# Projection banks asked for one at a time, a weight piece and zero products moved to the front, and a second early buffer for expert 2

## The reference

```python
def first_block(x, ...):
    hn = rms_norm(x, norm1_g)
    proj = hn @ w_in                       # 1024 -> 2304, the "projection" of this document
    # q and k are normed per head, some rotated; two attentions; w_out; conv FFN
    ...
def second_block(x, c, ctx, ...):
    # modulation by c, a scan and a windowed attention, then the experts:
    moe_x = hier_moe(h2, ...)              # 32 experts, 2 per token
    return rms_norm_2(x + g2 * moe_x, norm_final)

def expert_block(args):                    # for every expert e
    xb, e = args
    return (jax.nn.silu(xb @ w_gate[e]) * (xb @ w_up[e])) @ w_down[e]
```

## Time and profile before

| | us |
|---|---|
| median of 3 runs | 1606.25 (1605.87 to 1609.35) |
| the profiled execution | 1606.26 |
| its span on the chip | 1604.4 |
| PE busy | 1499.6 (93%) |

### The profile page before, as it was taken

One profiled execution on the slowest core, in us unless ns is written; L12 is line 12 of the kernel. 1 busy time (PEld: TensorE's weight loads), 2 busy tenths in 40 slices (PEclk: granted clock), 3 DMA queues, 4 the chain that ended last, 5 costly groups with the idle time before them and its releaser, 6 DMA issues.

```text
span 1604.4 us, 21206 instructions
## 1 busy us (share of the span) xinstructions
PE 1499.6 (93%) x8171; PEld 1041.4 (65%) x8171; DVE 913.7 (57%) x1697; ACT 518.9 (32%) x938; POOL 99.3 (6%) x132
## 2 busy tenths in 40 slices
PE   7999998999999999999999897988999999999896
PEld 6776667888888878878887686873444444344343
DVE  4745774467787567753764677472444454344435
ACT  5445665333343332243426534221101101010112
POOL 0000000000000000000004132001101101000100
PEclk9999998999999999999999999999999999999998
DMA  8212011255544357613020000565999999999993
GB/s 254 78 54 73 2 50 50 70 173 140 155 130 120 110 171 271 212 39 119 27 69 11 1 1 3 208 262 206 414 399 405 410 401 411 399 405 402 410 411 160
DMA packets 112365, 308.39 MB, mean 192 GB/s; under 512 B 13983, under 2 KB 65535, under 8 KB 90763
## 3 DMA queue, kind: packets, MB, share of 16 engines
q1 hardware_dynamic: 108755, 299.08, 50.4%
q0 software_dynamic: 3200, 7.87, 1.6%
q10 hardware_dynamic: 312, 0.10, 0.0%
HBM read 306.99 MB, written 4.22 MB: 194 GB/s over the span
## 4 chain that ended last, share of the span: by engine, by line
PE 73%; DMA 9%; DVE 8%; ACT 4%; issue 3%; SPq 2%; POOL 0%; DVEq 0%; ACTq 0%; POOLq 0%
PE bank L1309 68%; DMA arena<-in_w_up 8%; PE bank L1312 5%; SPq L826 1%; DVE arena L2192 1%; DVE ring L2134 0%; DVE hTc L2316 0%; ACT weights_high L971 0%; SPq L766 0%; DMA ring<-in_w_in 0%; DVE x_res L2205 0%; DVE ring L2136 0%; DVE xn L2204 0%; DVE arena L2386 0%; ACT hT_high L1031 0%
## 5 line engine op out<-in xcount | busy, mean ns | idle before, releaser
L1309 PE MATMUL bank<-weights_high,hT_high 128*128 128x512 f32 (+2 forms) x736 | 255.1, 385 | 12.6 <-ACT arena L1058 5.3
L1807 DVE TENSOR_TENSOR weights_low<-ring,weights_high 128x2048 fp32r<-128x2048 f32 (+2 forms) x61 | 135.6, 2224 | 139.8 <-ACT weights_high L971 138.9
L1309 PE MATMUL bank<-weights_low,hT_high 128*128 128x512 f32 (+2 forms) x560 | 212.6, 380 | 0.0
L971 ACT ACTIVATE weights_high<-ring 128x2048 fp32r<-128x2048 f32 (+2 forms) x61 | 113.4, 1859 | 190.7 <-PE bank L1309 158.0
L1309 PEld LDWEIGHTS bank<-weights_high,hT_high 128*128 128x128 f32 x736 | 139.0, 189 | 40.3 <-issue 8.4
L1309 PE MATMUL bank<-hT_high,weights_high 128*128 128x512 f32 x416 | 163.8, 394 | 0.8 <-DVE hT_low L1845 0.8
L1309 PE MATMUL bank<-hT_high,weights_low 128*128 128x512 f32 x416 | 161.9, 389 | 0.0
L1309 PE MATMUL bank<-hT_low,weights_high 128*128 128x512 f32 x416 | 161.9, 389 | 0.0
L2316 DVE TENSOR_TENSOR hTc<-bank,mod_gain 128x512 f32<-128x512 f32 x32 | 22.1, 691 | 193.9 <-PE bank L1312 193.9
L1309 PE MATMUL bank<-arena,hTc 128*64 128x512 f32 x496 | 115.6, 601 | 7.3 <-DMA arena<-in_w_up 5.7
L1309 PE MATMUL bank<-ring,hTc 128*64 128x512 f32 (+1 forms) x544 | 121.4, 583 | 0.6 <-DMA ring<-in_w_up 0.6
(11 more groups left out here) (329 smaller groups left out, 2483.7 us busy)
## 6 DMA issues: line engine op xcount, KB each, us to landing
arena<-in_w_up SPq DMA_DIRECT2D x32, 1024.0 KB, 20.0
arena<-in_w_down SPq DMA_DIRECT2D x16, 2048.0 KB, 22.3
ring<-in_w_gate SPq DMA_DIRECT2D x32, 1024.0 KB, 17.6
ring<-in_w_up SPq DMA_DIRECT2D x32, 1024.0 KB, 19.6
ring<-in_w_down SPq DMA_DIRECT2D x16, 2048.0 KB, 21.9
arena<-in_w_gate SPq DMA_DIRECT2D x30, 1024.0 KB, 18.6
xn<-in_w_ada SPq DMA_DIRECT2D x48, 512.0 KB, 4.7
ring<-in_w_up SPq DMA_DIRECT2D x44, 512.0 KB, 5.2
```

Of the source, the lines that this page charges most:

```text
L971: high_ready.tick(s.activation(part_view(w_high, key), raw_view(key), ACT.Copy), k)
L1309: return nc.tensor.matmul(o, lhsT, rhs, start=start, stop=stop)
L1807: low_ready.tick(v.tensor_tensor(part_view(w_low, key), raw_view(key), part_view(w_high, key), ALU.subtract), k)
```

## The change

Six edits. (1) The plan lists the projection's banks in the order in which they are first written, and PE opens each at its first matmul, not four together. (2) The nine products at n = 0 are gone. (3) POOL clears a 128x128 piece of `pj` at once, and PE multiplies it 15 times by itself before it waits for anything else. (4) SP issues the third weight piece after 10 of the small tables, ahead of the other 21. (5) Expert 2's up weights get a buffer of their own too (`early_up`, 16 KB per partition), loaded right after expert 1's weights and ahead of the store of the normed tokens; so expert 4's gate and up weights are loaded where expert 2's up weights were. (6) To make room, `ssd_small` lies in `early_up`, `convw` stands elsewhere, and the area for GpSimd's DMA descriptors is set to 4096 bytes.

```diff
+        early_up = sb("early_up", [P, UNIT])
...
+        sm = carve(0, 10, 96, of=early_up)
...
         for c in range(5):
             for n in range(4 * c, 4 * c + 4):
                 banks.plan(("proj", n), (pj_ready, n) if n < 16 else (v_tail, n - 16))
-
-            for n in range(4 * c - 2, 4 * c + 2):
-                if 0 <= n < 16:
+                if n % 2 and n >= 4:
+                    banks.plan(("qkT", 4 * c - 2 + n % 4 // 2), (qk_drained, 4 * c - 2 + n % 4 // 2))
+            if c < 4:
+                for n in range(4 * c, 4 * c + 2):
                     banks.plan(("qkT", n), (qk_drained, n))
...
                 if key == ("w_in", 1):
-                    for dst, src in small_loads[FIRST_LOADS:]:
+                    for dst, src in small_loads[FIRST_LOADS:FIRST_LOADS + 10]:
+                        sp.dma_start(dst, src).then_inc(more_in, 16)
+                if key == ("w_in", 2):
+                    for dst, src in small_loads[FIRST_LOADS + 10:]:
                         sp.dma_start(dst, src).then_inc(more_in, 16)
...
             load_expert(sp, 1, 1, None)
+            for half, landed in enumerate((first_in, second_in)):
+                sp.wait_ge(landed[1], 16)
+                load_rows(sp, 2, 0, 1, half, early_up[:, :])
             normed.wait(sp, ("norm2_2", TT - 1, 0))
             sp.dma_start(h_d.rearrange("(t p) n -> p t n", p=P), xn[:, 0:TT, :]).then_inc(h_stored, 16)
...
-            load_expert(sp, 2, 0, 1, True)
+            for landed in first_in[0:2] + second_in[0:2]:
+                sp.wait_ge(landed, 32)
+            load_gate_and_up(sp, 4, 0, 1)
+            load_down(sp, 2, 0, 1)
             load_expert(sp, 3, 1, 2)
             sp.wait_ge(gu_filled, 3)
             sp.dma_start(final_gain, inp["norm_final_2"].partition_broadcast(P)).then_inc(final_in, 16)
-            with sp.Fori(2, E // 2) as it:
+            load_down(sp, 4, 0, 3)
+            load_expert(sp, 5, 1, 4)
+            with sp.Fori(3, E // 2) as it:
...
+            g.memset(pj[:, 0, 0:P], 0.0).then_inc(zeros_ready, 1)
             banks.filled(pool, ("proj", len(PROJ) - 1))
...
+            opened = [banks.open(pe, ("hT",) + k) for k in halves("norm1")]
+            pe.wait_ge(zeros_ready, 1)
+            for _ in range(15):
+                mm(opened[0][:, 0:P], pj[:, 0, 0:P], pj[:, 0, 0:P], True, True)
             pe.wait_ge(const_in, CONST_ALL)
-            opened = [banks.open(pe, ("hT",) + k) for k in halves("norm1")]
...
                     bank = banks.open(pe, ("qkT", n))
-                    if n == 0:
-                        unread(bank, 9)
                     qk_ready.wait(pe, n)
...
-                opened = [banks.open(pe, ("proj", 4 * c + t)) for t in range(TT)] if c else []
+                opened = []
...
-                        if c == half == 0:
+                        if half == 0:
                             opened.append(banks.open(pe, ("proj", 4 * c + t)))
```

More of the change, by code:

```diff
@@ L195, in two_blocks @@
         gains = sb("gains", [P, 6, KT])
-        convw = sb("convw", [P, 224])
         ada_bias = sb("ada_bias", [P, 6, KT])
@@ L202, in two_blocks @@
         gates = sb("gates", [P, 2, D])
+        convw = sb("convw", [P, 224])
         dt_bias, a_log = sb("dt_bias", [P, 16]), sb("a_log", [P, 16])
@@ L294, in two_blocks @@
         skip_x = carve(2048 + 2 * (T + CTX), 512, of=slot)
-        sm = sb("ssd_small", [P, 10, 96])
         cat = xn
@@ L692, in two_blocks @@
         final_y = steps("final_y", range(TT))
+        zeros_ready = sem("zeros_ready")
         def pieces_of_turn(n):
@@ L766, in load_rows, with load_down, load_gate_and_up @@
             sp.dma_start(into[:, at], rows[:, at]).then_inc((first_in, second_in)[half][2 * par + i], 16)
-        def load_expert(sp, e, par, reuse, early=False):
+        def load_down(sp, e, par, reuse):
+            if reuse is not None:
+                sp.wait_ge(y_filled, reuse)
+            sp.dma_start(EXPERT_SLOTS[3 * par + 2], inp["w_down_2"].rearrange("a e (p f) d -> (a e) p (f d)", f=4)[e]).then_inc(
+                down_in[par], 16)
+        def load_gate_and_up(sp, e, par, reuse):
             if reuse is not None:
@@ L773, in load_expert @@
                 for i in range(2):
[L774 to L779, removed]
+                    load_rows(sp, e, par, i, half)
+        def load_expert(sp, e, par, reuse):
+            load_gate_and_up(sp, e, par, reuse)
+            load_down(sp, e, par, reuse)
         def modulation(sp, parts):
@@ L1709, in tokens_in_place, with gate_and_up @@
                 last.then_inc(xt_filled, 1)
-            def gate_and_up(n, par, kpar, gate=None):
-                gate_w, up_w = EXPERT_SLOTS[3 * par] if gate is None else gate, EXPERT_SLOTS[3 * par + 1]
+            def gate_and_up(n, par, kpar, early=None):
+                gate_w, up_w = EXPERT_SLOTS[3 * par:3 * par + 2] if early is None else early
                 pe.wait_ge(xt_ready, n + 1)
@@ L1774, in _ @@
                         pair_piece(pair, t)
-                gate_and_up(n, n % 2, n // 2, early_gate if n == 2 else None)
+                gate_and_up(n, n % 2, n // 2, (early_gate, early_up[:, :]) if n == 2 else None)
                 if n + 1 < E:
@@ L2399 @@
     from concourse.bass_utils import run_bass_kernel_spmd
-    nc = bacc.Bacc("TRN2", target_bir_lowering=False, num_devices=1)
+    nc = bacc.Bacc("TRN2", target_bir_lowering=False, num_devices=1, dynamic_dma_scratch_size=4096)
     arrays, aps = {}, {}
```

## The result

| | before | after |
|---|---|---|
| median of the runs | 1606.25 (5 runs, 1605.03 to 1609.35) | 1598.16 (5 runs, 1595.48 to 1598.88) |
| the profiled execution | 1606.26 | 1598.16 |
| its span | 1604.4 | 1596.2 |

The medians are 8.1 us apart, where 10.2 were forecast. The ratio of the runs is 0.9942, 95% interval 0.9931 to 0.9954; it is not simply the ratio of the medians, and stands for 9.3 us (7.4 to 11.1). So what has to be explained is not one number of 8.1 but a band from 8 to 12, and why it is so wide. The three intervals overlap, and the forecast of 10.2 us (0.9937) lies in all of them.

What follows compares the result with a forecast made beforehand. PE, busy 93% of the span, was taken to bound the kernel through its pauses in the first two thirds, the DMA weight stream in the last. Terms 6.8 + 0.2 + 0 + 3.2 = 10.2 us gave 1596.1 us, range 1592.8 to 1599.8.

Steps and rivals of the forecast that it cites:

- its own case: Whole kernel: the forecast's terms hold, 1596.1 us, range 1594.3 to 1598.0; chance 0.60.
- late tables: Rival: SP or DMA pushes the tables past 29 us, the pause at 38.18 grows, 1598.5 us; chance 0.09.
- Banks one by one: Projection: pauses at column blocks 2, 3 and 4 go (5.3 us), with block 2's slow clock (1.5): 6.8 us, bounds 5.3 to 7.0.
- Third piece and tables: Front: third weight piece ahead of 21 tables starts ACT 0.2 us earlier; bounds 2.7 us better, 1.5 worse.
- third high part: ACT's start on the third weight piece: forecast at 28.6 to 29, released by a table rather than the ring.
- DMA, not SP, is full there: Argument against late tables: while the small tables load, DMA is the limit rather than SP's issuing.
- Zero products: Start: 15 products before x let its transposes end up to 0.75 us earlier; costed at 0 unless tables come 4 us earlier.
- Nine products: Pause before the first head transposes: removing the fill costs 0, at most 1 us; by the skill's rule at most 1.5 us.
- Early up buffer: Experts: expert 2's up weights loaded early; queue runs dry at expert 5's gate, so 3.2 us, bounds 0 and 5.2.
- PE's waits for weights: Last third: PE waits for weights in 5 places, 5.7 us in all; forecast less than 3 us after.
- Sum: Whole kernel: 6.8 + 0.2 + 0 + 3.2 = 10.2 us, from 1606.25 to 1596.1 us.

Runs made afterwards that it cites:

- The three intervals: 95% intervals of the changed kernel's ratio to the kernel before, from three measurements: 0.9931 to 0.9954, 0.9909 to 0.9938, 0.9916 to 0.9943.
- the two later ones: Medians of the same changed kernel, unedited, measured again on two chips beside the kernel before: 1595.29 (ratio 0.9923) and 1595.12 (0.993).
- the third profile: The changed kernel, nothing edited, profiled a third time: span 1593.3 us; runs on that chip 1595.12 us, 0.993 of the kernel before.
- the split tables: Changed kernel, but ACT and DVE wait ahead of product 0 only for the 12 tables used there: 1595.09 us (0.9922), on another chip 1595.78 (0.9938).

## Why the prediction was right, and where its terms were off

The mechanisms of the two large terms, the banks and the buffer, were right: the banks are shown by themselves, the buffer by itself and by its absence. That the first median, 1598.16, lies 2 us above the forecast and the two later ones 1 us below it is in part luck: the terms as measured give 10 to 11 us, and the middle of the execution, in which nothing was forecast, moves by 4. The first median is just outside the range that the prediction gave its own case (up to 1598.0) and beside the 1598.5 of late tables, but the tables were not late: the last one landed at 28.9, inside the 28.6 to 29.0 of the forecast.

- **Banks one by one**, 6.8 us (5.3 to 7.0): right in mechanism, 7.6 measured, above the upper bound. Two sizes were small. An idle time in brackets counts from the modelled end of the work ahead of it. Ahead of each of the three pauses stand four transposes; before, those of block 2:

```profile
66.89 0.63 PE L1312 MATMUL bank<-const,arena 128*128 128x128 f32 x4
```

  Their row is 0.63 us long, but where nothing waits, the next matmul starts 0.39 after their start (67.20 and 67.59 above). In the same way a matmul of 512 columns is shown as 0.39 us while the next starts 0.23 after it (27.27, 27.50). So one pause loses about 0.24 us more than its bracket, and three make 5.3 + 0.7. And the half-clock stretch costs half of its 3.4 us, 1.7 and not 1.5. That makes 7.7. The first part is worked out from the rows and not tried by itself.
- **Third piece and tables**, 0.2 us: 0.2 in the profile. Over all profiles the third high part starts at 29.8 on the mean of five with the late piece, at 28.8 on the mean of six with the early one and the undivided wait, so up to 1.0 (the starts of x alone scatter by as much). The step behind the number is not borne out: I had written that DMA, not SP, is full there. The stretches of the earlier trace rows in the changed kernel, and some of SP's issues:

```profile
15.00:22.00 7.00, 7.00 (x32) 5.80 (x31) 5.63 (x8) 6.93 (x12) 0.00 (x0) 1.00 0.83 251
22.00:26.00 4.00, 4.00 (x19) 3.30 (x19) 0.33 (x2) 2.46 (x6) 0.00 (x0) 1.00 0.87 252
26.00:29.00 3.00, 3.00 (x15) 2.49 (x14) 0.13 (x1) 0.13 (x1) 0.00 (x0) 1.00 0.93 105
```

```profile
14.61 2.53 SPq L839 DMA_DIRECT2D arena<-in_conv_w  x2
...
20.36 2.07 SPq L839 DMA_DIRECT2D gates<-in_b_ada  x2
...
25.97 0.73 SPq L839 DMA_DIRECT2D route_w<-in_w_expert  x1
26.74 6.85 SPq L833 DMA_DIRECT2D ring<-in_w_in  x2
```

  The share has gone down from 1.04 to 0.83 between 15 and 22 (0.97 in the third profile). The last table is issued at 25.97 (before 22.11) and lands 2.9 us behind that (before 4.3), so its time follows the issue. But two pairs of tables take SP 2.53 and 2.07 us, against 0.77 and 0.91 before, and what held SP there is not shown; a queue filled by the piece would do it too. Whether SP or DMA is the limit stays open. (The semaphore of the tables covers 30 of them, 10 ahead of the piece and 20 behind it, not 31 and 21.)
- **Zero products**, 0 behind a late table and up to 0.75 with early ones: 0 and 1.0.
- **Nine products**, 0 with 1 us on the bad side: 0 as far as the runs tell. By the rule of the Trainium skill that the prediction cites, this pause of 5.2 us would have cost another stretch. The stretch did become twice as long, but so it did with the nine products (pause of 3.57 us), and in the kernel without the buffer (4.54 us) it did not. Before, a pause of 2.17 us had a single stretch in one profile and one of 2.45 us none in the other. The rows neither bear the rule out nor refute it.
- **Early up buffer**, 3.2 us (3.4 worked out): 3.4 in the stream, 3.2 and 3.7 in the runs. The queue that runs dry at the gate of expert 5 and its restart were the right reason for less than 5.2: the last landing ahead of the gate's load and its own are 6.1 us apart (1138.1, 1144.2), before 3.0 (1148.6, 1151.6). One reason was wrong: PE's waits for weights, which I wanted to see below 3 us, stay at 3.2 to 6.0 in the profiles of after. They need not shrink, since the whole end moves with the stream.
- **Sum**, 10.2 us: the terms as measured, 7.6 + 0.2 + 3.4 less 0.2 to 1.2 for the long stretch at 35 us, give 10.0 to 11.0, inside the band of 8.1 to 11.5. What is missing in the profile first compared is in the middle, which takes 4.2 us, while the end gives 1.7. The lead of ACT's events over before is 7.4 us at 226 and falls in steps: to 5.9 at 264, to 4.4 at 709, to 3.5 at 928, to 3.1 at the first gate. At the second and third step the changed kernel has a stretch at 694 where before has none, and a double one at 912 where before has one at 919, in code that is the same. At the first both kernels have stretches, before even one more (247 to 262 against 240 to 258). In all, the middle has 27.3 us at half clock against 23.9, which could cost 1.7 us and not 4.2; the third profile of the changed kernel has the same 27.3 and loses 1.3. So what counts is also where a stretch falls, and the steps show where the 4.2 us went but not that half clock alone took them.

What stays open is why the lead of the split tables, 4.4 us at 122 us and 3.6 at the first gate, is not seen in the runs. It would need profiles of the slower half of its runs.

## What to carry to other kernels

Cut every profile at a few fixed events and compare the pieces over several kernels: here two of five pieces carried the change to some 1 us, while the whole span hid it in a scatter of 4. Where an instruction waits for two things that come at nearly the same time, moving one of them gives next to nothing (third high part at 28.87 or 29.77 with one moved, 25.02 with both); look at what comes next before pricing the move, and ask of the later one whether its issuer or its transfer is the limit. A bank, or any resource in a ring, should be asked for at its first use and planned in that order.

## What the runs showed of the hardware

- The place of TensorE's half-clock stretches, mostly 3.4 us each, is not a property of the program: same instructions, 0.1 us of difference at 55 us, and a stretch at 694 is there or not. One costs 1.7 us on full work: the 16 products of the last down take 5.35 us with it and 3.65 without. The profiled executions have a mean granted clock of 0.974 to 0.983, which is some 52 to 83 us at half clock each. The spans of one kernel's three profiles differ by 3.5 us, and its runs by 4.5 on one chip.
- A stretch in which PE waits for another engine anyway costs nothing: the projection of before takes 100.2 us with stretches at 39 and 70 and 100.1 with one at 72.
- From the first gate of the experts the stream of weights takes 475.5 to 477.2 us in eight profiles with the early buffer, wherever PE's stretches fall. The last piece is 25.5 to 25.6 us in five profiles with a stretch in the last down product, and 23.7 to 24.4 in seven without.
